# x and mem also read features first, the small vectors in two tables, the first chunk by blocks of 128 rows

## The reference

```python
# first block
h = rms_norm(x, attn_norm_g)             # y = x * rsqrt(mean(x*x) + 1e-6), then * g
proj = h @ w_in                          # 1024 x 5128: qa, ka, va, qb, kb, vb, forget, gates
qa = partial_rope(rms_norm(heads(qa), moba_q_norm_g), pos); ka likewise
# MoBA attention on a, forgetting attention on b, gates, w_out, a gated FFN with a 3-tap convolution
# second block
mem_n = rmsnorm(mem_2, norm_mem_2)
km, vm = split(mem_n @ w_mem_kv_2, 2)    # 1024 x 512; keys and values of 4 memory heads
# HGRN2 mix, top-k attention, attention on the memory, w_out_2, a second gated FFN
```

## Time and profile before

| | |
|---|---|
| runs | 743.37, 746.51, 742.42 us; median 743.37 |
| profiled execution, span from first to last instruction | 742.2 us (the page gives no other time for it) |
| TensorE busy | 730.1 us, 98% |
| VectorE, ScalarE busy | 506.7 and 480.7 us, 68% and 65% |
| moved by DMA | 128.61 MB, 173 GB/s in the mean |
| chain that ended last | 88% TensorE, 4% VectorE, 4% DMA, 3% ScalarE |

### The profile page before, as it was taken

How to read it: one execution, slowest core, us unless ns; L and a number is a source line. 1 busy time by engine, 2 the same in 40 slices (tenths; PEclk the granted TensorE clock), 3 DMA queues, 4 the chain that set the end, 5 groups by cost and what they waited for, 6 DMA issues and landing times.

```text
span 742.2 us, 10606 instructions
## 1 busy us (share of the span) xinstructions
PE 730.1 (98%) x3788; PEld 604.3 (81%) x3788; DVE 506.7 (68%) x777; ACT 480.7 (65%) x763; POOL 8.4 (1%) x18
## 2 busy tenths in 40 slices
PE   8999999999999999999999999999899999999998
PEld 5888898887788888888888888877688888888886
DVE  5785787667776878677555567999877765567540
ACT  6775777866357787776533886777957776557420
POOL 0003000000000000000000000000000000000000
PEclk9999999999999999999999999999999999999999
DMA  8684745445557654546763644511176755566630
GB/s 323 219 267 145 224 145 169 127 144 155 158 157 240 226 197 146 177 160 226 242 195 109 212 140 128 163 37 58 59 225 207 238 181 168 170 225 222 208 109 28
DMA packets 70460, 128.61 MB, mean 173 GB/s; under 512 B 4915, under 2 KB 17044, under 8 KB 70420
## 3 DMA queue, kind: packets, MB, share of 16 engines
q1 hardware_dynamic: 69684, 125.62, 52.8%
q10 hardware_dynamic: 736, 2.46, 1.1%
HBM read 127.02 MB, written 1.05 MB: 173 GB/s over the span
## 4 chain that ended last, share of the span: by engine, by line
PE 88%; DVE 4%; DMA 4%; ACT 3%; issue 1%; SPq 0%; ACTq 0%; DVEq 0%
PE acc L597 26%; PE acc L599 25%; PE acc L598 25%; DVE b_wlo L1571 2%; DMA b_raw<-in_w_ffn_up 2%; PE banks L619 1%; PE banks L737 1%; PE banks L632 1%; DMA b_gates<-in_mem 1%; PE banks L915 1%; ACT b_whi L1076 1%; PE banks L664 1%; DMA b_raw<-in_w_in 1%; PE banks L649 1%; PE banks L778 1%
## 5 line engine op out<-in xcount | busy, mean ns | idle before, releaser
L1571 DVE TENSOR_TENSOR b_wlo<-b_raw,b_whi 128x1024 fp32r<-128x1024 f32 (+4 forms) x232 | 267.7, 1186 | 90.0 <-ACT b_whi L1076 89.5
L1076 ACT ACTIVATE b_whi<-b_raw 128x1024 fp32r<-128x1024 f32 (+4 forms) x232 | 232.5, 1029 | 91.8 <-PE acc L599 34.1
L597 PE MATMUL acc<-b_whi,b_hhi 128*128 128x512 f32 (+4 forms) x512 | 198.2, 387 | 0.4 <-DVE b_hlo L1880 0.4
L599 PE MATMUL acc<-b_wlo,b_hhi 128*128 128x512 f32 (+4 forms) x512 | 193.6, 378 | 0.0
L598 PE MATMUL acc<-b_whi,b_hlo 128*128 128x512 f32 (+4 forms) x512 | 193.3, 378 | 0.0
L597 PEld LDWEIGHTS acc<-b_whi,b_hhi 128*128 128x128 f32 x512 | 96.3, 188 | 18.5 <-issue 2.0
L599 PEld LDWEIGHTS acc<-b_wlo,b_hhi 128*128 128x128 f32 x512 | 96.2, 188 | 16.2
L598 PEld LDWEIGHTS acc<-b_whi,b_hlo 128*128 128x128 f32 x512 | 96.4, 188 | 14.6
L597 PE MATMUL acc<-b_whi,b_ohi 128*128 128x512 f32 x256 | 102.7, 401 | 0.5 <-DVE b_wlo L1571 0.5
L599 PE MATMUL acc<-b_wlo,b_ohi 128*128 128x512 f32 x256 | 100.3, 392 | 0.0
L598 PE MATMUL acc<-b_whi,b_olo 128*128 128x512 f32 x256 | 100.2, 392 | 0.0
(11 more groups left out here) (263 smaller groups left out, 745.5 us busy)
## 6 DMA issues: line engine op xcount, KB each, us to landing
b_raw<-in_w_in SPq DMA_DIRECT2D x48, 512.0 KB, 4.5
b_raw<-in_w_ffn_up SPq DMA_DIRECT2D x40, 512.0 KB, 4.6
b_raw<-in_w_ffn_in SPq DMA_DIRECT2D x40, 512.0 KB, 4.6
b_raw<-in_w_ffn_down SPq DMA_DIRECT2D x22, 512.0 KB, 5.4
b_raw<-in_w_ffn_out SPq DMA_DIRECT2D x22, 512.0 KB, 4.4
b_raw<-in_w_out SPq DMA_DIRECT2D x16, 512.0 KB, 3.8
b_raw<-in_w_in SPq DMA_DIRECT2D x12, 412.0 KB, 4.7
b_raw<-in_w_in SPq DMA_DIRECT2D x8, 410.0 KB, 3.9
```

The source lines that it names most:

```text
L597: nc.tensor.matmul(o, a, wh, start=first, stop=False)
L599: mm = nc.tensor.matmul(o, a, wl, start=False, stop=last)
L1076: ins = A(whi[:, n % SPLIT, 0:c["nk"], 0:c["n"]], raw[:, n % RAW, 0:c["nk"], 0:c["n"]], ACT.Copy)
L1571: ins = V.tensor_tensor(wlo[:, n % SPLIT, 0:c["nk"], 0:c["n"]], raw[:, n % RAW, 0:c["nk"], 0:c["n"]], whi[:, n % SPLIT, 0:c["nk"], 0:c["n" ...
```

## The change

- x and mem_2 are given in a second form, already transposed (xT, memT: 1024 x 256). They come by DMA features first in pieces of 128 or 256 features, whose rows are 1 KB long. ScalarE rounds the high part with the gain as a scale per partition ("in hi"), VectorE makes the low part ("in lo"), per block of 128 features. The transposes of mem and x, their evictions, the products of x with its gain and the scaled split of the mkv weights go away.
- The token forms of x and mem_2 are still loaded, for the squares, and later in SyncE's order.
- The small vectors come in two tables: the columns (110 numbers per partition, one DMA at the start on ScalarE's queue) and the constants, to which the head gains and the forget bias are added (one DMA of 1000 numbers per partition, behind chunk 9). No small DMAs are left, and the turn of the vectors goes.
- The first chunk is split by blocks of 128 rows ("first hi", "first lo", first_chunk), so that its first six matmuls need only the first block of weights and of mem.
- The two instructions on ones now follow each other at once.

```diff
@@ tables: the starts of the three lists (the rest keeps its order, less the turns, evictions and gains)
-ORDER1["pe"] = [("norm turn", "mem", 0, 0), ("norm turn", "mem", 1, 0), ("norm turn", "mem", 0, 1), ("gemm", "mkv", 0, 0),
...
+ORDER1["pe"] = [("gemm", "mkv", 0), ("gemm", "mkv", 1, 0), ("gemm", "mkv", 1, 1), ("gemm", "mkv", 2, 0), ("gemm", "mkv", 3, 0),
...
@@ TensorE
+            def first_chunk(name):
+                g = groups[name]
+                hi, lo = lhs_of[g["lhs"]]
+                for k in range(CK):
+                    pe.wait_ge(*at("in hi", f"{TURNED[name]} {k}"))
+                    pe.wait_ge(sem("first hi" if k == 0 else "hi ready"), 1)
+                    for t in range(T):
+                        nc.tensor.matmul(acc[0][t][:, 0:g["n"]], hi[:, k, t * P:(t + 1) * P], whi[:, 0, k, 0:g["n"]],
+                                         start=k == 0, stop=False)
+                    pe.wait_ge(*at("in lo", f"{TURNED[name]} {k}"))
...
+                    pe.wait_ge(sem("first lo" if k == 0 else "lo ready"), 1)
...
+                if name in TURNED and t == 0:
+                    pe.wait_ge(*at("in lo", f"{TURNED[name]} {2 * c + 1}"))
-            idle(1)
-            pe.wait_ge(sem("identity in"), 16)
-            gain_column()
-            idle(1)
+            idle(2)
@@ SyncE
-            memory(0, 0)
...
+            turned("mem", 0)
             for n, c in enumerate(chunks):
-                if n == 1:
-                    memory(0, 1)
-                elif n == 2:
-                    memory(1, 0)
-                    memory(1, 1)
+                if 0 < n < RAW:
+                    turned("mem", n + 1)
                 if n == RAW:
-                    sp.dma_start(gain[:, :], dram["attn_norm_g"][0, :].partition_broadcast(P))\
-                      .then_inc(sem("gain in"), 16)
-                    for _ in tokens(x, "x", "x"):
-                        pass
-                if n > RAW + 2:
-                    next(constants, None)
-                    next(constants, None)
+                    turned("x1", 0)
+                    turned("x1", 1)
+                elif RAW < n < 2 * RAW:
+                    turned("x1", n - RAW + 1)
+                if n == RAW + 1:
+                    tokens(memx, "mem_2", "mem", 0)
+                    tokens(memx, "mem_2", "mem", 1)
+                elif n == 2 * RAW:
+                    tokens(x, "x", "x", 0)
+                elif n == 2 * RAW + 1:
+                    tokens(x, "x", "x", 1)
+                elif n == 2 * RAW + 2:
+                    sp.dma_start(cst[:, :], dram["consts"]).then_inc(sem("consts in"), 16)
@@ ScalarE
-            act.dma_start(ident, dram["consts"][:, C_ID:C_ID + P]).then_inc(sem("identity in"), 16)
-            act.dma_start(memg, dram["norm_mem_2"][0, :].rearrange("(k p) -> k p", p=P)).then_inc(sem("mem gain row in"), 16)
+            act.dma_start(param[:, :], dram["cols"]).then_inc(sem("columns in"), 16)
...
+            def in_hi(which, k):
+                if (which, k) == ("mem", 0):
+                    act.wait_ge(sem("columns in"), 16)
+                act.wait_ge(sem(f"{which}T {piece_of(k)} in"), 16)
+                done(A(SIDE[which][0][:, k, :], turned_in(which, k), ACT.Copy, scale=norm_column(which, k)),
+                     "in hi", f"{which} {k}")
@@ VectorE
+            def in_lo(which, k):
+                dve.wait_ge(*at("in hi", f"{which} {k}"))
+                hi, lo = SIDE[which]
+                done(V.scalar_tensor_tensor(lo[:, k, :], turned_in(which, k), norm_column(which, k),
+                                            hi[:, k, :].bitcast(F32), ALU.mult, ALU.subtract), "in lo", f"{which} {k}")
```

More of the change, by code:

```diff
@@ new lines @@
+ORDER1["act"] = [("in hi", "mem", 0), ("first hi", "mkv"), ("in hi", "mem", 1), ("hi", "mkv", 0), ("in hi", "mem", 2, 3),
+     ("hi", "mkv", 1), ("in hi", "mem", 4, 5), ("hi", "mkv", 2), ("in hi", "mem", 6, 7), ("hi", "mkv", 3),
+     ("in hi", "x1", 0, 1), ("hi", "qa", 0), ("norm squares", "mem", 0), ("norm squares", "mem", 1),
+     ("norm guess", "mem"), ("in hi", "x1", 2, 3), ("hi", "qa", 1), ("in hi", "x1", 4, 5), ("hi", "qa", 2),
+     ("in hi", "x1", 6, 7), ("norm squares", "x1", 0), ("norm squares", "x1", 1), ("sums", "mkv", 0),
[9 rows of a table added]
+     ("pv", 2), ("scores", 4), ("probs", 3), ("sums", "vb", 0), ("gate log", "fg2"), ("mix", 0), ("pv", 3),
+     ("sums", "vb", 1), ("scores", 5), ("hi", "bra1", 0), ("probs", 4), ("mix", 1), ("next gain", "x1"),
[7 rows of a table added]
@@ L612, in norm_T @@
             def norm_T(k, b, tiles=range(T)):
[L614 removed]
                 for t in tiles:
[L616 removed]
+                    pe.wait_ge(*at("tokens scaled", f"{k} {t} {b}"))
                     claim(2 * t + b, f"{k}T")
@@ L808, in ffn2 @@
                         chunk("d2_1", c, t)
-            def gain_column():
-                pe.wait_ge(sem("mem gain row in"), 16)
-                nc.tensor.transpose(acc[1][0][:, 0:KT], memg, ident[0:KT, 0:KT]).then_inc(sem("mem gain turned"), 1)
             def idle(n):
@@ new lines, in turned @@
+            def turned(which, piece):
+                for k in range(PIECES[piece].start, PIECES[piece].stop, 2):
+                    ks = slice(k, min(k + 2, PIECES[piece].stop))
+                    n = ks.stop - ks.start
+                    dst = xT[:, ks, :] if which == "x1" else \
+                        gates[:, k // 4, D + k % 4 * S:D + (k % 4 + n) * S].rearrange("p (k s) -> p k s", s=S)
+                    src = dram["xT" if which == "x1" else "memT"][k * P:(k + n) * P, :]
+                    sp.dma_start(dst, src.rearrange("(k p) s -> p k s", p=P)).then_inc(sem(f"{which}T {piece} in"), 16)
@@ L1014, in _ @@
                         if g == 0:
-                            for bank in range(2 * T):
-                                sp.wait_ge(*at(f"bank{bank} full", "memT"))
+                            sp.wait_ge(*at("in lo", "mem 7"))
                             sp.wait_ge(*at("squares", "mem 1"))
@@ L1035, in _ @@
                           .then_inc(sem("first rows in"), 16)
+                        turned("mem", 1)
                         k0 = 1
@@ L1364, in merged_hi @@
                            X[2 * t + c].rearrange("p (c t) -> p c t", t=P), ACT.Copy), "merged hi", f"{c} {t}")
-            act.wait_ge(sem("mem gain turned"), 1)
-            done(A(gcol[:, :], acc[1][0][:, 0:KT], ACT.Copy), "mem gain column", "0")
-            act.wait_ge(*at("mem gain column", "0"))
             where = {"mk": mkT, "qa": qT[0], "ka": kT[0], "qb": qT[1], "kb": kT[1]}
@@ L1372, in _ @@
                     hi_to(groups[n]["at"][rest[0]])
+                elif kind == "first hi":
+                    first_hi(n)
+                elif kind == "in hi":
+                    for k in rest:
+                        in_hi(n, k)
                 elif kind[:4] == "norm":
@@ L1885, in _ @@
                     lo_to(groups[n]["at"][rest[0]])
+                elif kind == "first lo":
+                    first_lo(n)
+                elif kind == "in lo":
+                    for k in rest:
+                        in_lo(n, k)
                 elif kind[:4] == "norm":
```

240 lines of the change are left out of this document (110 added, 130 removed), and 70 rows, old and new, of the table pick.

## The result

The changed kernel takes 749.9 us (median of four runs, 747.8 to 750.7) against 743.35 us: ratio 1.0083, 95% interval 1.0062 to 1.0104, or 6.2 us slower. I had forecast 744.7 us with a range up to 748.0; the time lies above it. The profiled execution has a span of 746.0 us, the shortest of the four (the others 747.4 to 748.9), against 742.2. Two runs further down, one of e8 (810.23 us at a granted clock of 0.85) and one of the kernel before beside it (913.29 us), are left out of the ratios.

A forecast was written before the change was run, and what follows sets the result against it. TensorE, busy 730.1 of 742.2 us, was taken to bound the kernel. Profiled span 742.2 + 0.2 + 1.2 - 0.1 = 743.5 us, plus 1.2 us from span to median: 744.7 us (0.60), range 741.5 to 748.0.

The forecast's parts named there:

- The start: First weight-chunk matmul at 5.5 us in place of 10.70, chunk 1 at 11.7 us; the five microseconds' gain not kept.
- The landing of x: Second half of x's tokens, late in SyncE's transfer order, lands at 28.8 us, bounds 26.8 to 31.5.
- The 1.2 us for rows of 1 KB: Extra transfer time in x's landing: 2.1 MB in short rows at 325 in place of 398 GB/s.
- My reading of the row at 541 us: 228 GB/s at 541 to 551 us taken as the cost of 1 KB rows, scaled to 325 GB/s.
- Chunk 7: Last chunk of qa, ready 4.8 us after x lands, at 33.6 us; TensorE idles 3.3 us before it; term +0.2 us.
- The bank of va: Second wait: va's bank, held by qa's tile 0, free at 41.6 us; TensorE wants it at 40.4; +1.2 us.
- The clock, rival 2: Idle gaps around chunk 7 lower TensorE's clock, 1.7 us per fall: one fall 746.4 us (0.17), two 748.1 (0.09).
- 1.9 us were too short for it: In the kernel before, waits behind the start up to 1.9 us did not lower TensorE's clock.
- Everything behind 45 us unchanged: After the bank of va TensorE's work keeps its old length, except 0.1 us less for the small vectors' turn.
- The offset: Median of the runs taken to lie 1.2 us over the profiled span, added to 743.5 us.
- 1.3 us for the start: Sum of the terms on the profiled execution: +0.2 (chunk 7), +1.2 (bank of va), -0.1 (small vectors' turn).

The follow-up runs named there:

- e8: Changed kernel with 96 unused bytes, last qa and first ka chunk's parts before x's squares, constants later, two matmuls on ones behind the first chunk; 746.95 us.
- e7: Changed kernel without the blocks of 128 rows on TensorE: the first chunk waits for both parts and goes tile by tile; 749.13 us, ratio 1.0073.
- e3: Changed kernel with three float32 matmuls on ones into a free bank in front of chunk 7; 749.86 us, ratio 1.0093.
- e6: Kernel before with 64 unused bytes per partition in front of the tiles of the phases; 747.63 us, ratio 1.0045.
- e5: Changed kernel with 96 unused bytes per partition in front of the tiles of the phases; 749.24 us, ratio 1.0069.
- e2: Kernel before with 32 unused bytes per partition ahead of the tiles of the first phase; 746.65 us, ratio 1.0053.
- e9: Changed kernel with 224 unused bytes per partition in front of the tiles of the phases; 746.35 us, ratio 1.0031.
- e11: e8 with 224 unused bytes instead, mk's guess and heads and one low part earlier, tokens of mem and x requested and squared later; 741.97 us, ratio 0.9977.

## Why the prediction was wrong

Step by step:

- **The start.** First matmul forecast at 5.5 us, measured 4.72; chunk 1 at 11.7, measured 10.78. That this gain is not kept was right, and e7 shows it.
- **The landing of x.** Forecast 28.8 us (26.8 to 31.5), measured 27.6. The 1.2 us for rows of 1 KB were not there in the landing: with such rows in it, the stretch from 8 to 27 us moves 385 GB/s against the 398 of the earlier trace rows, which is 0.6 us over its 19 us. The Trainium skill (DMA: Bandwidth & Descriptors, Specifications) says that rows from 512 B on reach line rate, and this trace agrees to within those 3%. My reading of the row at 541 us was wrong: a queue that isn't kept full may explain it as well as short rows, for the window from 541 to 551 us of the changed kernel has 278 GB/s in place of 228.
- **Chunk 7.** 4.8 us behind the landing: forecast 33.6, measured 32.70, 5.1 us behind. The idle time of 3.3 us was measured at 3.34.
- **The bank of va.** Forecast: free at 41.6, TensorE 1.4 us late there. Measured: 41.21 us, 1.04 us late, without a wait.
- **The clock, rival 2.** It fell, twice: behind a gap of 2.27 us and one of 3.34 us. The mechanism and the 1.7 us were right. But I added its price to the wait for the bank, and in the profiled execution the two cover each other: TensorE reached va slowly, at 41.21 us, and found the bank free since 41.04. In e3 the fall is gone and the wait is there, 1.10 us, where I had put 1.2. The Trainium skill (TensorE: Matmul & The Clock Gate, What's actually happening) says that idleness puts the array back to 1.2 GHz; the trace agrees behind both gaps. But that 1.9 us were too short for it, as I read in the earlier trace rows, holds for some executions and not for others. e6, the kernel before with 64 unused bytes, has the same wait of 1.85 us and is slow behind it. Here are the transposes behind the wait in e6, then those in the kernel before, then e6's stretch behind the wait with its granted clock of 0.57:

```profile
528.46 1.54 PE L707 MATMUL banks<-b_cst,b_gain 128*128 128x128 f32 x6 [1.85 <-ACT b_gain L1206]
```
```profile
526.63 0.88 PE L705 MATMUL banks<-b_cst,b_gain 128*128 128x128 f32 x6 [1.85 <-ACT b_gain L1204]
```
```profile
528.00:532.00 4.00, 3.54 (x12) 2.90 (x12) 3.80 (x12) 3.81 (x12) 0.00 (x0) 0.57 0.00 0
```

  The traces of e5, e7 and e8 have a fall at this place too, with a granted clock of 0.57 over the 4 us behind the same wait.
- **Everything behind 45 us unchanged: this is the step that failed.** "All I have to find out is how much earlier TensorE arrives at the point where it again never waits", says the prediction, and its sum ends at the bank of va: it puts what TensorE does behind that at its old length, without a reason. In the profiled pair TensorE is 1.0 us late at 41 us and 0.4 us at 342 us, and then loses 3.4 us in the 528 matmuls of the down projections, by the place of their stationary tiles. e2 shows the cause by itself in the kernel before (+3.9 us), e9 takes it away in the changed one (6.2 us slower becomes 2.3 us, interval 1.2 to 3.3). No rival of mine had it.
- **The offset.** I took the runs to lie 1.2 us over the span. In every run that has both, time less span is 1.8 to 1.9 us, so the profiled execution of before took 744.0 us: 0.6 us too low.

For the profiled pair the sum closes: 742.2 + 0.4 (what is left of the start at 342 us) + 3.4 (528 x 6.4 ns) = 746.0 us. The forecast had 1.3 us for the start, so 0.9 too much there. The median of the runs lies 2.1 us above the profiled one (749.9 against 747.8), and with the 0.6 us of the offset this makes up the miss: 0.6 + 3.4 - 0.9 + 2.1 = 5.2 us.

The 2.1 us go with the clock. In the traces a run with one slow stretch has a mean granted clock of 0.998 (e6), with two 0.995 (the changed kernel), with three 0.993 (e9, whose second stretch, from 33 us on, is twice as long and counts double). The runs, by this number (mean time in us, count; two readings of before and one each of e9 and e11 lie in between and are left out):

| kernel | 1.000 | 0.998 | 0.995 | 0.993 |
|---|---|---|---|---|
| before, beside e9 | 743.1 (22) | 744.4 (8) | 744.5 (3) | |
| changed | | | 748.5 (2) | 750.6 (2) |
| e9 | | 745.1 (1) | 745.2 (4) | 747.0 (6) |
| e11 | 739.9 (3) | 742.1 (5) | 744.1 (3) | |

So rival 2 was worth more than its chances said: the changed kernel falls two or three times, and the third fall goes with about 2 us. Of all 68 runs of the kernel before, beside the experiments, 34 have no fall and 25 have one. In e9 the third fall raises the mean by 0.9 us (746.1 in all, 745.2 in the five runs with one or two), and the 1.5 us by which those five lie above the kernel before (743.7 in the mean) are near the 1.3 us forecast for the start. Where the third fall of the two slower runs of the changed kernel lies is not on record (behind chunk 7 as in e9, or at 529 us as in e5), and no kernel takes it away by itself; that stays open.

## What to carry to other kernels

Before a change that resizes or removes tiles is read by its schedule, compare the start addresses of all matmul operands: a tile that moves by some bytes can change the pace of work that the diff never touches. Unused bytes in front of the tiles show it in a run or two; to find the right number took three tries here (32, 96 and 224). An engine that starts earlier gains only up to the next thing that arrives by a saturated queue; ask at each later wait what ends it, and let no transfer or instruction stand in front that isn't needed yet. Two delays at neighbouring places (a slow clock, a bank that isn't free) are not to be added before it is clear that one does not hide the other. One trace shows the clock of one execution: before it is read as what a kernel does, compare the mean granted clock of all its runs.

## What the runs showed of the hardware

- The distance between matmuls of 128x128 fp32 weights on a moving 128x512 is 226.9 ns when the stationary and the moving tile start at the same remainder modulo 256, and 232.6 to 233.4 ns with the stationary one at 0, 160 or 192 and the moving one at 128 (160 and 192 at two starts each). Which operand's read is in the way, and other types, were not tried.
- TensorE's clock fell to the 1.2 GHz level behind gaps of 2.27 and 3.34 us in the changed kernel. Behind the same wait of 1.85 us it stayed up in the traces of the kernel before and the changed one and fell in those of e5, e6, e7 and e8.
- Where the wait for a transfer ends did not depend on when TensorE began: with the first chunk 2.4 us later (e7), chunk 7 started at the same time within 0.1 us.
